# A reordered expert stage: PE's transposes of the activated block moved behind the gate-and-up matmuls, a DVE copy moved behind a multiply, and one early row gather moved behind a weight gather

## The reference

```python
    flat_e = expert_ids.reshape(A).astype(jnp.int32)        # A = 1024 * 2
    order = jnp.argsort(flat_e)
    ...
    padded = ((counts + ROW_BLK - 1) // ROW_BLK) * ROW_BLK  # ROW_BLK = 128
    ...
    n_blocks = A // ROW_BLK + N_EXPERTS
    rows = x_pad[row_tok].reshape(n_blocks, ROW_BLK, D)

    def block_ffn(args):
        xb, e = args
        return (jax.nn.silu(xb @ w_gate[e]) * (xb @ w_up[e])) @ w_down[e]

    ys = lax.map(block_ffn, (rows, block_expert)).reshape(P, D) * row_w[:, None]
    out = jnp.zeros((n_tok + 1, D), ys.dtype).at[row_tok].add(ys)[:n_tok]
```

## Time and profile before

| | |
|---|---|
| median of three runs | 3788.63 us |
| the profiled execution | 3788.63 us |
| its span, first to last instruction | 3787.3 us |
| PE busy | 3509.3 us (93%) |
| DVE, ACT, POOL busy | 1296.0, 907.8, 285.9 us |
| granted TensorE clock, mean over the span | 0.964 |
| expert stage | about 3149 us (first weight gather) to 3707 us (last matmul) |

### The profile page before, as it was taken

One profiled execution on the slowest core, in us unless ns is written; L12 is line 12 of the kernel. 1 busy time (PEld: TensorE's weight loads), 2 busy tenths in 40 slices (PEclk: granted clock), 3 DMA queues, 4 the chain that ended last, 5 costly groups with the idle time before them and its releaser, 6 DMA issues.

```text
span 3787.3 us, 30826 instructions
## 1 busy us (share of the span) xinstructions
PE 3509.3 (93%) x12602; PEld 1929.9 (51%) x12602; DVE 1296.0 (34%) x2346; ACT 907.8 (24%) x1742; POOL 285.9 (8%) x258
## 2 busy tenths in 40 slices
PE   9999998899988999999999999999789997999991
PEld 6458546666643444444444456765356534444440
DVE  5445476466612111111000023214556223221116
ACT  3110453477722100000000012112334131111112
POOL 0002131000000000000000000000000002222214
PEclk8999999999999999999999999999999998999995
DMA  5114212000021110100010100002000107999984
GB/s 208 45 62 156 95 67 98 3 1 1 1 100 56 34 44 34 45 34 32 33 38 31 69 23 29 35 8 89 11 1 23 45 18 301 373 366 368 369 319 161
DMA packets 60936, 362.17 MB, mean 96 GB/s; under 512 B 6570, under 2 KB 12986, under 8 KB 35196
## 3 DMA queue, kind: packets, MB, share of 16 engines
q1 hardware_dynamic: 38188, 179.32, 13.0%
q0 software_dynamic: 22608, 180.89, 12.7%
HBM read 324.97 MB, written 35.22 MB: 95 GB/s over the span
## 4 chain that ended last, share of the span: by engine, by line
PE 83%; DVE 8%; ACT 7%; issue 1%; DMA 1%; POOL 0%; SPq 0%; DVEq 0%; ACTq 0%; POOLq 0%
PE ps L1237 16%; PE ps L2328 9%; PE ps L1284 8%; PE ps L1393 6%; PE ps L2347 4%; PE ps L807 3%; PE ps L1987 3%; PE ps L1182 3%; PE ps L1395 3%; PE ps L954 2%; PE ps L673 2%; PE ps L810 2%; PE ps L982 2%; PE ps L616 1%; ACT arena L1034 1%; PE ps L1827 1%
## 5 line engine op out<-in xcount | busy, mean ns | idle before, releaser
L1237 PE MATMUL ps<-arena 128*128 128x512 f32 x1408 | 607.4, 594 | 5.0 <-ACT arena L1223 5.0
L1237 PEld LDWEIGHTS ps<-arena 128*128 128x128 f32 x1408 | 268.5, 191 | 343.7 <-issue 337.9
L2328 PE MATMUL ps<-arena 128*128 128x512 f32 x752 | 332.6, 595 | 0.0
L1284 PE MATMUL ps<-arena 128*128 128x512 f32 x704 | 302.6, 592 | 1.4 <-DVE arena L1270 1.4
L2286 POOL DMA_INDIRECT arena<-in_wgu_dram,arena x47 | 44.2, 941 | 2784.6 <-DVE arena L2247 2530.0
L2328 PEld LDWEIGHTS ps<-arena 128*128 128x128 f32 x752 | 140.1, 191 | 158.7 <-issue 158.7
L1284 PEld LDWEIGHTS ps<-arena 128*128 128x128 f32 x704 | 132.9, 189 | 171.2 <-issue 169.0
L1393 PE MATMUL ps<-arena 128*128 128x512 f32 x480 | 210.8, 600 | 0.0
L1089 DVE TENSOR_SCALAR_CACHE_REDUCE arena<-ps 128x1280 f32<-128x1280 f32 x96 | 139.2, 1488 | 110.0 <-PE ps L954 110.0
L807 PE MATMUL ps<-arena 128*128 128x512 f32 (+1 forms) x432 | 174.7, 558 | 0.0
L2347 PE MATMUL ps<-arena 128*128 128x512 f32 x376 | 169.1, 592 | 0.5 <-DVE arena L2396 0.5
(11 more groups left out here) (346 smaller groups left out, 4777.4 us busy)
## 6 DMA issues: line engine op xcount, KB each, us to landing
arena<-in_wmod_dram SPq DMA_DIRECT2D x24, 1024.0 KB, 5.4
yslot<-arena SPq DMA_DIRECT2D x47, 512.0 KB, 8.5
arena<-in_wup_dram SPq DMA_DIRECT2D x22, 1024.0 KB, 4.8
arena<-in_wout_dram SPq DMA_DIRECT2D x16, 1024.0 KB, 4.8
arena<-in_cf_dram SPq DMA_DIRECT2D x12, 1024.0 KB, 4.8
arena<-in_wdn_dram SPq DMA_DIRECT2D x16, 704.0 KB, 4.1
arena<-in_w2b_dram SPq DMA_DIRECT2D x9, 1024.0 KB, 4.8
arena<-in_ci_dram SPq DMA_DIRECT2D x16, 512.0 KB, 3.5
```

What stands on the lines that cost most here:

```text
L1237: ins = mm(bk(b + tc), sb(wat(n) + k * 256 + which * 128, 128), sb(HT + k * 1024 + tc * 512, 512), k == 0, k == 7)
L1284: ins = mm(bk(bs[tc]), sb(wat(n) + k * 128, 128), sb(GB + (11 * hh + k) * 1024 + tc * 512, 512), hh == 0 and k == 0, hh == 1 and k == 10)
L2328: ins = mm(bk(b), sb(XB + i % 2 * 1024 + k * 128, 128), sb(WGU[i % 3] + k * 512, 512), k == 0, k == 7)
```

## The change

Three orders are changed, on PE, on DVE and on POOL. No instruction is added, removed or resized.

```diff
--- before.py
+++ after.py
@@ -2303,8 +2303,8 @@
         for j in range(8):
             G.wait_ge(*(yield ("xd", j)))
         yield from pool_rows(0)
+        yield from pool_weights(1)
         yield from pool_rows(1)
-        yield from pool_weights(1)
         for i in range(2, NBLK):
             yield from pool_rows(i)
             yield from pool_weights(i)
@@ -2329,7 +2329,7 @@
         ins.then_inc(*P.step(("egu", i)))
         held[b] = [("eh", i)]
 
-    def pe_eht(i):
+    def pe_edn(i):
         b = 4 + i % 2
         yield from claim(b)
         P.wait_ge(*(yield ("eh", i)))
@@ -2337,8 +2337,6 @@
             ins = turn(bk(b, 128, off=k * 128), sb(HB + i % 2 * 256 + k * 128, 128), ident)
         ins.then_inc(*P.step(("eht", i)))
         held[b] = [("ehc", i)]
-
-    def pe_edn(i):
         P.wait_ge(*(yield ("ehc", i)))
         P.wait_ge(*(yield ("wed", i)))
         for h2 in range(2):
@@ -2352,8 +2350,6 @@
         for i in range(NBLK + 2):
             if i < NBLK:
                 yield from pe_ex(i)
-            if i >= 2:
-                yield from pe_eht(i - 2)
             if 1 <= i <= NBLK:
                 yield from pe_egu(i - 1)
             if i >= 2:
@@ -2389,16 +2385,15 @@
                     V.wait_ge(*(yield ("egu", i - 2)))
                 V.wait_ge(*(yield ("ex", i, 0)))
                 vt.tensor_copy(sb(XB + i % 2 * 1024, 512), bk(0)).then_inc(*V.step(("xb", i, 0)))
+            if 1 <= i <= NBLK:
+                h = sb(HB + (i - 1) % 2 * 256, 256)
+                V.wait_ge(*(yield ("esilu", i - 1)))
+                vt.tensor_tensor(h, h, bk(2 + (i - 1) % 2, 256, off=256), MUL).then_inc(*V.step(("eh", i - 1)))
             if i >= 2:
                 V.wait_ge(*(yield ("eht", i - 2)))
                 if i > 3:
                     V.wait_ge(*(yield ("edn", i - 4)))
                 vt.tensor_copy(sb(HB + 512 + i % 2 * 256, 256), bk(4 + i % 2, 256)).then_inc(*V.step(("ehc", i - 2)))
-            if 1 <= i <= NBLK:
-                h = sb(HB + (i - 1) % 2 * 256, 256)
-                V.wait_ge(*(yield ("esilu", i - 1)))
-                vt.tensor_tensor(h, h, bk(2 + (i - 1) % 2, 256, off=256), MUL).then_inc(*V.step(("eh", i - 1)))
-            if i >= 2:
                 V.wait_ge(*(yield ("ey", i - 2, 0)))
                 if i > 3:
                     V.wait_ge(*(yield ("ys", i - 4)))
```

## The result

| | before | changed |
|---|---|---|
| median | 3788.63 us (4 runs, 3788.38 to 3789.14) | 3857.77 us (4 runs, 3855.78 to 3861.45) |
| profiled execution | 3788.63 us, span 3787.3 | 3859.38 us, span 3857.2 |
| changed to before | | 1.0183, 95% interval 1.0166 to 1.0201 |

The change made the kernel 69 us slower; 3856 us was forecast, in a range of 3843 to 3868.

A forecast was written before the change was run, and what follows sets the result against it. The prediction took PE's own sequence to bound the expert stage. To 3788.6 us it added 59.8 for 46 longer blocks and 7.3 for the late start, giving 3855.7, say 3856 us, in a range of 3843 to 3868.

The forecast's parts named there:

- PE paces the stage: Expert stage: PE's own sequence is the path, 11.39 us a block; the DMA engines follow at 368 GB/s.
- The block's growth, 1.30 us: Each expert block: the uncovered eht-copy-edn round trip costs 1.52 us less eht's 0.22, giving 12.69 us a block.
- four pieces of the working: After egu, T being the next matmul's start: multiply T+0.61, copy T+0.94, edn T+1.42, its eight matmuls 3.70 us.
- The lower bound of the term, 0.78 us a block: Block growth if the copy came at T+0.42, not held by the multiply: 36 us in all; as a rival, chance 0.04.
- The count, 46: Iterations 2 to 47 have both an egu and an edn, so the block's growth counts 46 times, 59.8 us.
- The clock at nothing: PE's clock in the blocks: gaps of about 1.1 us leave it at 1.00; rival of a falling clock, chance 0.03.
- The start, 7.3 us: Start of the expert stage: rows(1), issued behind 3.1 MB of weights, lands at 3175.55, making ex(1) 7.3 us late.
- the 11.1 taken from wed: Landing time assumed for rows(1) in fourth place: wed(1), there before, landed 11.1 us after its issue.
- Nothing gives the 7.3 us back: Start of the expert stage: the 7.3 us delay stays in full, as PE paces the stage.
- The whole: Whole kernel: 3788.6 + 59.8 + 7.3 = 3855.7 us, say 3856.
- The 0.5 us by which runs of this kernel were said to differ: Whole kernel: claimed run-to-run difference of 0.5 us, with 0.2%, 7.6 us, counted as a difference.

The follow-up runs named there:

- half-depth run: Kernel before with edn at half its depth, one of two matmuls for each half of the result, all transfers kept: 3720.28 us, one run.
- Reordering the start: Kernel before with PE taking egu(0) ahead of ex(1): 3791.52 us, ratio 1.0005.

## Why the prediction was right

- **PE paces the stage.** Held. The waits told it, and the half-depth run shows where the other bound lies.
- **The block's growth, 1.30 us.** Measured 12.71 - 11.39 = 1.32 in the chain, and 60.0 us for the second part of the stage, against 59.8. All four pieces of the working were met: multiply T+0.62 (0.61), copy T+0.96 (0.94), edn T+1.43 (1.42), eight matmuls 3.70 us. The lower bound of the term, 0.78 us a block, is what PE's edit costs alone.
- **The count, 46.** Held; the last block was uncovered before, as said.
- **The clock at nothing.** Held: 1.00 beside gaps of 1.04 us and of 1.50.
- **The start, 7.3 us.** The mechanism held: the rows landed behind the 3.1 MB of weights, 11.9 us after their issue (12.2 with POOL's edit alone) and not 6.2, as order within the queue has it. That the number is met to the tenth is luck. Two errors cancel in this pair of traces: the rows landed 0.8 us later than the 11.1 taken from wed, and the clock, which the prediction lets shift with the rest, rose sooner after ex(1), so that from ex(1) to ex(2) it is 10.07 us (3178.59 to 3188.66) against 10.74, 0.7 us less. "Nothing gives the 7.3 us back" is wrong by that much in this pair, but the clock's rise scatters with no edit at all: egu(0) took 7.58 to 9.16 us in the five traces with POOL's order of before, and 7.98 to 8.50 in the four with the changed one. The trace of before that the prediction was read from has the longest start of the five, 14.04 us. Over all of them the means of ex(0) to ex(2) are 13.0 and 21.3 us, and the term is 8.3. Why the gather of rows lands 0.8 to 1.1 us later than wed did in the same place was not tested.
- **The whole.** 3855.7 forecast, 3857.8 and 3857.3 measured. In the profiled run the stage has 67.4 us of a span 69.9 us longer; 2.3 us lie ahead of it. The 0.5 us by which runs of this kernel were said to differ was too little: in the later sessions the kernel before took 3786.7 to 3795.8 us. An agreement of the whole to 2 us is thus better than the forecast could know.
- **What the prediction left out.** It put the loss down to eht's move and let DVE's order add to it. The DVE edit is the costlier of the two, and does more damage by itself than both together.

## What to carry to other kernels

A software pipeline is one order written on several engines: here one stage taken one slot late, on PE or on DVE, uncovered the round trip, however early the other was. Price such a wait from a place where the trace shows it uncovered, here the last block, and then ask what has come to stand ahead of it in the queue of the engine that answers. For a stage in which compute and transfers both look full, read which of them has waits before believing a bandwidth figure. And before an effect of 1 or 2 us is put down to an edit, compare it with the same stretch in traces where nothing in it was changed.

## What the runs showed that was not expected

DVE's edit alone was expected from the first traces but not in the prediction: 68.3 us for an exchange of two instructions, 0.42 us each. The rise of the clock isn't tied to the first matmuls after an idle stretch by a fixed delay: after ex(1) it took 6.0 us before, 3.2 with DVE's edit alone, whose instructions up to there stand in the same order, and 3.6 with POOL's edit alone. Reordering the start moved 1.36 us of waiting to three other places and doubled it, in part through a table load of 1.28 us that had cost nothing where it stood in the kernel before.
